# A two-layer decoder trunk: the first layer's mixer in two token halves, the second half beside the expert retrieval

## The reference

```python
h = rmsnorm(x, norm_mix[0])                     # layer 0
u, v, q, kc, vc, ks, vs, kw, vw, gt = split(h @ w_in)
a = chunked_gmlp(gelu(u), gelu(v), ...)         # chunks of 128 tokens, causal inside
b = nsa(q, kc, vc, ks, vs, kw, vw, gt, ...)     # 8 heads, causal: compressed, selected and window branch
x = x + concatenate([a, b]) @ w_out
x = x + peer(rmsnorm(x, norm_ffn[0]))           # retrieval
x = x + odd_mixer(rmsnorm(x, norm_mix[1]))      # layer 1: gated linear recurrence, state from chunk to chunk
x = x + peer(rmsnorm(x, norm_ffn[1]))
out = rmsnorm(x, final_norm)

def peer(xb):                                   # per token: 8 heads, top 16 of 128 x 128 expert pairs
    s = (xb @ w_q) . sub_keys; experts = top16(top16(s[0]) + top16(s[1])); gate = softmax(best)
    act = gelu(xb . u_tab[experts])
    return sum(gate * act * v_tab[experts])
```

## Time and profile before

| | us |
|---|---|
| median of 3 runs | 3397.39 (3396.7 to 3400.4) |
| the profiled execution | 3394.91 |
| its span, first to last instruction | 3392.7 |
| start to the first dot product | 543.2 |
| slots 0 to 255 | 690.1 |
| slots 256 to 511, 512 to 767 | 754.4, 744.5 |
| slots 768 to 1023 and the end | 660.5 |
| PE, DVE, ACT, POOL busy | 2912.1, 2225.1, 1450.8, 1272.0 |

### The profile page before, as it was taken

One profiled execution on the slowest core, in us unless ns is written; L12 is line 12 of the kernel. 1 busy time (PEld: TensorE's weight loads), 2 busy tenths in 40 slices (PEclk: granted clock), 3 DMA queues, 4 the chain that ended last, 5 costly groups with the idle time before them and its releaser, 6 DMA issues.

```text
span 3392.7 us, 30594 instructions
## 1 busy us (share of the span) xinstructions
PE 2912.1 (86%) x8568; PEld 1544.7 (46%) x8568; DVE 2225.1 (66%) x5636; ACT 1450.8 (43%) x3950; POOL 1272.0 (37%) x1254
## 2 busy tenths in 40 slices
PE   7988888887898879898998978988989887787787
PEld 3655655442344435555545545555545532222222
DVE  1134415666766677888886678888886676667664
ACT  0022212444444446555544346555644444444443
POOL 2000003343443444444444344545454344444442
PEclk9865579999999999999999999999999999999999
DMA  4110007999999999999999999999999999999997
GB/s 169 63 42 0 1 7 304 415 415 419 396 414 414 421 411 415 377 376 382 390 401 412 412 411 420 369 387 383 391 403 412 410 417 422 421 421 406 422 421 325
DMA packets 198202, 1178.72 MB, mean 347 GB/s; under 512 B 20368, under 2 KB 57488, under 8 KB 61456
## 3 DMA queue, kind: packets, MB, share of 16 engines
q0 software_dynamic: 147456, 1073.81, 77.6%
q1 hardware_dynamic: 50576, 102.96, 8.1%
HBM read 1173.55 MB, written 2.10 MB: 347 GB/s over the span
## 4 chain that ended last, share of the span: by engine, by line
PE 44%; DMA 29%; DVE 13%; ACT 7%; issue 4%; POOL 2%; SPq 0%; DVEq 0%; POOLq 0%; ACTq 0%
DMA region_g<-in_uv_dram,experts 26%; PE ps L1566 20%; DVE region_g L1153 6%; PE ps L1400 5%; DMA region_a<-in_keys_dram 3%; PE ps L1437 2%; PE ps L1348 2%; PE ps L1251 2%; PE ps L1310 2%; PE ps L1362 2%; PE ps L1238 2%; POOL region_g L568 1%; PE ps L1338 1%; ACT x_res L780 1%; PE ps L1434 1%
## 5 line engine op out<-in xcount | busy, mean ns | idle before, releaser
L1566 PE MATMUL ps<-region_g,x_res 128*128 128x512 f32 x3840 | 1875.4, 621 | 333.0 <-ACT x_res L780 303.3
L568 POOL DMA_INDIRECT region_g<-in_uv_dram,experts x1024 | 1142.2, 1115 | 1614.7 <-PE ps L1566 1355.5
L1153 DVE CUSTOM_DVE_ANT_0 region_g<-region_g,region_h 128x1024 f32<-128x1024 f32 x1024 | 1255.2, 1228 | 579.5 <-DMA region_g<-in_uv_dram,experts 568.5
L1566 PEld LDWEIGHTS ps<-region_g,x_res 128*128 128x128 f32 x3840 | 706.5, 195 | 1249.9 <-ACT x_res L780 622.1
L773 ACT ACTIVATE region_a<-region_a 128x1 f32<-128x1 f32 x1024 | 207.0, 202 | 1360.2 <-DVE region_a L1153 1357.0
L780 ACT ACTIVATE x_res<-ident_z,region_a 128x128 f32<-128x128 f32 x960 | 385.4, 401 | 31.4
L774 ACT ACTIVATE region_a<-region_a,gate 128x1 f32<-128x1 f32 x1024 | 301.5, 294 | 33.3
L1400 PE MATMUL ps<-region_a 128*128 128x256 f32 x1024 | 243.7, 383 | 8.5 <-DMA region_a<-in_keys_dram 7.3
L1400 PEld LDWEIGHTS ps<-region_a 128*128 128x128 f32 x1024 | 196.5, 192 | 86.2 <-issue 55.1
L773 ACT ACT_TABLE_LOAD x110 | 141.1, 1283 | 6.8 <-DVE region_a L1153 4.9
L1434 PE MATMUL ps<-region_a 128*128 128x256 f32 x512 | 133.3, 391 | 1.0 <-DVE region_a L993 1.0
(11 more groups left out here) (221 smaller groups left out, 2469.9 us busy)
## 6 DMA issues: line engine op xcount, KB each, us to landing
region_a<-in_w_q_dram SPq DMA_DIRECT2D x32, 1024.0 KB
region_a<-in_w_odd_dram SPq DMA_DIRECT2D x32, 1024.0 KB
region_g<-in_uv_dram,experts POOLq DMA_INDIRECT x1024
region_a<-in_w_out_o_dram SPq DMA_DIRECT2D x8, 1024.0 KB
region_a<-in_w_even_dram SPq DMA_DIRECT2D x1, 5216.0 KB, 19.9
region_a<-in_w_even_dram SPq DMA_DIRECT2D x1, 4096.0 KB, 16.4
region_g<-in_w_out_e_dram SPq DMA_DIRECT2D x1, 4096.0 KB, 13.5
region_a<-in_keys_dram SPq DMA_DIRECT2D x32, 128.0 KB
```

What stands on the lines that cost most here:

```text
L568: g.indirect_dma_start(out=gath[:, s % NBUF, :], out_offset=None, in_=uv[s // (2 * PHASE)], in_offset=bass.IndirectOffsetOnAxis(ap=experts ...
L1153: v.tensor_tensor_reduce(out=u_, in0=u_, in1=XNr[n // P_HEADS % 3], scale=1.0, scalar=0.0, op0=ALU.mult, op1=ALU.add, accum_out=dots[:, c: ...
L1566: i = t.matmul(PS[:, j, :], diag[:, pe_n(s) % NBUF, :], gath[:, s % NBUF, D_MODEL + j * 512:D_MODEL + (j + 1) * 512], start=first, stop=last)
```

## The change

The first layer's mixer is written as generators too (`even_pieces(q)` on each engine), for one half of 256 tokens each: q = 0 stands ahead of the retrieval, q = 1 begins at tick 0, with its attention from tick 102 (`ATT`) to about 170 and its output projection at ticks 150 to 178. The routing of the first half keeps its ticks (heads 2 to 7 every 14 slots), that of the second moves from tick 130 on (heads every 13 slots) to tick 182 on (every 7). `Threads` merges mixer and routing by tick.

- Weights come as slabs of 256 columns, 1 to 1.2 MB: seven buffers in region_g for q = 0, for q = 1 the three in region_a that the routing uses too, in order of ticks. A slab is loaded when the one three before has been used. `w_even` slabs and `w_q` slabs have pieces of 1 KB, the compression's and output's of 8 KB.
- Attention: 16 units for each half. The probabilities are scaled by their gates and sums ahead of the transposes (ACT, `scaled`), the transposes of both branches go through one PSUM bank (6) one behind the other, and the value products are transposed: 256 columns, two heads at once, all branches added in PSUM, with no combination on DVE.
- The compression's position is a third plane of the same products (first half), and the loop stands twice.
- The routing has one PSUM bank for queries (4) and one for scores (5), instead of two each.
- POOL's level masks are built at ticks 122 to 136; its other constants early in q = 0. `DVE_ROWS` stays.

```diff
+UNITS = 16
+ATT = 102
+EVEN_AT = (-1000, 0)
...
-        NORM_TICK = (-100, 130, PHASE + NORM_AT, 2 * PHASE + NORM_AT)
+        NORM_TICK = (-100, ATT + 80, PHASE + NORM_AT, 2 * PHASE + NORM_AT)
...
-            if job == 1:
-                return 140 + 13 * h
             return NORM_TICK[job] + 9 + 7 * h
...
+        def even_slabs(q):
+            t = EVEN_AT[q]
+            out_ = [(t + 12 + 8 * i, ("F", q, i), (f_done, 4 * q + i)) for i in range(4)]
+            out_ += [(t + 44, ("G", q), (g_done, q))]
+            out_ += [(t + 52 + 8 * kv, ("C", q, kv), ((c_half, q), (hid_done, q))[kv]) for kv in range(2)]
+            out_ += [(t + 68 + 8 * i, ("V", q, i), ((v_half, q), (v_done, 2 * q + 1))[i]) for i in range(2)]
+            out_ += [(t + 84 + 8 * i, ("U", q, i), ((u_half, q), (u_done, 2 * q + 1))[i]) for i in range(2)]
+            return out_ + output_slabs(q, t + ATT + 48)
...
+        order_ = even_slabs(1) + routing_slabs(0) + routing_slabs(1)
...
+        order_.sort(key=lambda e: e[0])
```

ACT, in `even_pieces(q)`:

```diff
+                for step in range(2, 4 * UNITS + 8, 2):
+                    yield t0 + ATT + step
...
+                    if step % 4 == 0:
+                        if step >= 8:
+                            probabilities_out(q, step // 4 - 2, 1)
+                        if step // 4 <= UNITS:
+                            scaled(q, step // 4 - 1)
+                    else:
...
+                            probabilities_out(q, (step - 6) // 4, 0)
+                        if step // 4 < UNITS:
+                            exponentials(q, step // 4)
```

PE, in `even_pieces(q)` and the functions it calls:

```diff
+                yield t0 + ATT
+                scores(q, 0)
...
+                for step in range(4, 4 * UNITS + 8, 2):
+                    yield t0 + ATT + step
+                    u = step // 4
+                    if step % 4 == 0:
+                        if u < UNITS:
+                            scores(q, u)
+                        if step >= 12 and u % 2 == 1:
+                            values(q, u - 2)
+                        if 1 <= u <= UNITS:
+                            probability_transposes(q, u - 1, 0)
+                    elif step >= 6 and u - 1 < UNITS:
+                        probability_transposes(q, u - 1, 1)
+                        if (u - 1) % 2 == 1:
+                            compressed_transposes(q, u - 1)
...
+            def probability_transposes(q, u, br):
...
+                if br == 0:
+                    pe.wait_ge(ps_ready.sem, ps_ready.at(n))
...
+                after(pe, pT_out, 2 * n + br - 1)
+                for kt in range(2 * q + r + 1):
+                    i = t.transpose(PS[:, 6, kt * P:(kt + 1) * P], zs[:, u % 2, br, kt * P:(kt + 1) * P], ident)
+                i.then_inc(pT_done.sem, 1)
...
+            def values(q, u):
...
+                for br in range(2):
+                    for kt in range(2 * q + r + 1):
+                        t.matmul(PS[own, 7, 0:HALF], vsw[:, kt, br, own], pT[:, br, kt, :],
+                                 start=br == 0 and kt == 0, stop=False)
+                t.matmul(PS[own, 7, 0:HALF], vcmp[:, own], pcT, start=False, stop=True).then_inc(pv_done.sem, 1)
```

More of the change, by code:

```diff
@@ L556, in mixer_pieces, with mixers, routings @@
                     small_root(final_ss[:, b:b + 1], final_rstd[:, b:b + 1], 1).then_inc(f_rs.sem, 1)
+            def mixers():
+                yield from even_pieces(0)
+                yield from even_pieces(1)
+                yield from level_masks()
+                for q in range(2):
+                    yield from odd_pieces(q)
+                yield from final_pieces()
+            def routings():
+                for job in range(4):
+                    yield from routing_pieces(job)
+            threads = Threads(mixers(), routings())
+            threads.run(-80)
+            pool.wait_ge(pw_done.sem, pw_done.at(3))
             link.reset()
[L559 to L561 removed]
             for s in range(SLOTS):
@@ new lines, in compressed_transposes @@
+            def compressed_transposes(q, u):
+                n = UNITS * q + u
+                pair, r, e, _ = unit(u)
+                pe.wait_ge(pc_ready.sem, pc_ready.at(q))
+                pe.wait_ge(aT_out.sem, aT_out.at(2 * q))
+                after(pe, pcT_out, n // 2 - 1)
+                for c in range(2):
+                    m = B_HEADS * r + head_of(e, 2 * pair + c)
+                    i = t.transpose(PS[0:N_CMP, 7, HALF + c * P:HALF + (c + 1) * P], pc[:, m * N_CMP:(m + 1) * N_CMP], ident)
+                i.then_inc(pcT_done.sem, 1)
```

1347 lines of the change are left out of this document (718 added, 629 removed).

## The result

The changed kernel takes **3196.1 us** (median of 4 runs, 3185.7 to 3202.1) against 3397.5 for the kernel before: a ratio of **0.940** (95% interval 0.938 to 0.943), 201 us faster. Direction and main mechanism held; three terms of the sum were clearly too large (the part before the retrieval, rows 180 to 255, and rows 256 on), and the last of them for a reason that has nothing to do with the mixer.

A forecast was written before the change was run, and what follows sets the result against it. DMA was taken to bound the retrieval rows while idling in the mixer before them. First dot product 273.5, first 256 rows 819 and the rest 2159.4 gave a span of 3252, forecast 3256.5 us, range 3205 to 3325.

The forecast's parts named there:

- First dot product: Half the mixer before the retrieval: retrieval's first dot product at 273.5 us, 269.7 sooner than before, give or take 20.
- Rows 0 to 101: Second half's norm, projections and compression beside the first 102 retrieval rows: 3.3 us a row, 337 us, bounds 315 and 367.
- with two so close the sum is more than either: Rows 0 to 101: PE at 3.09 and DMA at 2.93 us a row together cost more, taken as 3.3.
- packed sum: PE's work in a woven stretch, added without gaps at 2.4 GHz; 306 us, 3.00 a row, in rows 0 to 101.
- rival (a): First 102 rows: the slab queue binds, at 25 us a slab 395 us in place of 337, total 3314; chance 0.17.
- signs of being wrong: First 256 rows under 750 us, PE waiting for slabs by tens of microseconds, or attention before the retrieval at 2.4 GHz.
- Rows 102 to 179: Second half's attention and output projection beside 78 rows, PE and ACT nearly full and tied: 253 us, bounds 234 and 289.
- Rival (b): Woven attention: ACT binds beyond PE if a table switch costs twice 1.28 us; 3.65 a row, total 3285; chance 0.07.
- Rows 180 to 255: Eight routing heads every 7 rows instead of 13: 56 rows at 3.1 us and 20 at 2.75, 229 us.
- Rows 256 on: Same work in the same order as the kernel before: 2159.4 us, bounds 0 and 10 more.
- Rival (c): Cleaner overlap: first 256 rows in 767 us and the first part 18 us sooner, total 3187; chance 0.14.

The follow-up runs named there:

- narrow: Changed kernel with the first token half's value products issued as two of 128 columns in place of one of 256: 3195.3 us, ratio 0.942.
- contig: Changed kernel with first-layer weight and routing query slabs laid out in DRAM as one 8 KB piece per partition: 3154.5 us, ratio 0.929.
- after_ra: Changed kernel with the gathers' buffers moved by 384 bytes, to 1024 bytes beyond their place in the kernel before: 3225.3 us, ratio 0.948.
- contig_ra: contig with its first buffer region 96 elements larger, gathers' buffers 1024 bytes beyond their place in the kernel before: 3175.6 us, ratio 0.935.
- contig_ra1152: contig with its gathers' buffers 1152 bytes beyond their place in the kernel before: 3157.7 us, ratio 0.929.

## Why the prediction missed, step by step

- **First dot product, 273.5, measured 257.0.** Two steps failed. The attention began at 105 and not 112: the start at 17.6 (19 forecast), features 29.7 (28.4), token projections 37.9 (36.6) and compression 12.5 (12) were right, but 16 us were added for small products and for waits beside which nothing ran, and only 7 were there. And attention and output projection took 108 us (105 to 213.1) in place of 120: 90.7 for 101 up to 195.7 us, 17.4 for 19 behind it. The clock had been forecast at the lower level through the attention, with 2 us for its rise after it; it had a mean of 0.68 in the attention and was at 1.00 behind it, where no time went into a rise. By narrow the values' wide products are worth 2 to 3 of these 12 us. The rest fits the time from 168 us on, when pieces of the output projection stand between the units and the clock is high in both kernels; what raised it there was not tested. From the projection's end to the first dot product 43.9 us, forecast 41.5.
- **Rows 0 to 101, 337, measured 331.0: right size, wrong make.** The step that failed is the surcharge "with two so close the sum is more than either": 3.3 a row on a packed sum of 3.00. Without the slabs' waits (contig) the rows took 303.0 us against that packed sum of 306. What filled the difference in the changed kernel was rival (a), which I had priced at 58 us, with every slab late: three were, and they cost 28. One of the prediction's own signs of being wrong thus came true: PE waited for slabs by tens of microseconds, 22.1.
- **Rows 102 to 179, 253, measured 247.3.** Mechanism and size held: PE and ACT, each nearly full, tied by waits. Rival (b) fell, at least for its price: without 32 table loads ACT's busy time went from 182.1 to 140.0 us, and the rows gave 5.4.
- **Rows 180 to 255, 229, measured 211.7.** The packed sum was right again (2.86 a row in 56 rows) and its surcharge wrong: I divided by a clock of 0.97, where the stretch had 0.99, and went to 3.1 after rows 448 to 511 of the kernel before, which took 2.90 on a slow address and with slabs of 1 KB pieces. In the changed kernel those rows take 2.86 and in contig 2.80. From the packed sum, 56 x 2.86 + 20 x 2.75 = 215.
- **Rows 256 on, 2159.4, measured 2145.4.** "The same work in the same order" was true of the instructions, not of their buffers. On the old address class (after_ra) it was 2167.5, within the 10 us that were allowed.
- **In sum.** after_ra has the span 3224.6: of the 60 us, 32 are the address, 15 the part before the retrieval, 20 the woven rows, less 8 behind row 256. Rival (c) named nearly the right time, 3187, but not for its reason: the woven rows took 790 us, not 767, and of its 18 us in front, which were 16.5, 7 came from small products and waits that weren't there, 12 from the faster attention and projection, of which narrow leaves the values' 256 columns 2 to 3, and 2 were lost again behind the projection. That the time came near it is luck: 32 us of it are the address, which no rival had. Two sums of the prediction are off by under 1 us: 45.2 - 10 + 6 is 41.2, not 41.5, and 64 x 3.2 + 14 x 3.4 is 252, not 253.

On the slabs, the Trainium skill (DMA: Bandwidth & Descriptors, Queues, rings and completion order) was cited for DMA engines that go round their queues a packet at a time, by which small pieces stay slow as long as the gathers are full. The landings agree (24 to 33 us behind three slabs in 1 KB pieces, a median of 12.0 behind slabs in one piece); the packets' order itself shows in no run.

## What to carry to other kernels

Price a woven stretch by the packed sum of each engine first, and add a surcharge only where two engines wait for each other in program order; here a DMA at its full 414 GB/s beside a PE that was busy 0.98 added nothing to PE's packed sum (303.0 us for 306). An engine that looks full in the trace is shown to be the bound only when taking work from it shortens the stretch, and where two are tied, take from both at once. When a change moves buffers, ask whether its gain is the order or the addresses: pad the old kernel to the new addresses and run it.

## What was not expected of the hardware

- The start address of the gathers' buffers changes their rate by 1.5%: in the slices of the page where nothing stands beside them, 421 GB/s at 0, 768 and 1024 bytes from the old place, 427 at 640 and 1152. The landing of a gather, from the DMA issues of contig_ra and of contig_ra1152:

```profile
region_g<-in_uv_dram,experts POOLq DMA_INDIRECT x1024, 13.3
```

```profile
region_g<-in_uv_dram,experts POOLq DMA_INDIRECT x1024, 12.4
```

- A megabyte in eight pieces of 1 KB a partition, with its keys behind it, landed beside the gathers 24 to 33 us after its issue in three places of the changed kernel; in one piece of 8 KB a partition the slab landed after 9.5 us and the keys behind it after 12.0 (medians).
- One late slab costs PE twice: the wait, and the first eight MATMULs after it at half the clock (3.78 in place of 1.73 us).
